# A two-layer gMLP and attention trunk on one core: the first norm's weights spread by matmuls, the root table loaded first, row tiles turned sooner, attention in another order

## What is computed

```python
for l in range(DEPTH):
    h = rms_norm(x, pre_mix_g[l])
    z = h @ w_in[l]                       # columns: u | v | q | k | value
    uv = gelu(z[..., :o_q])               # u, v_g = halves of uv
    y_a = gmlp_mixer(u, v_g, ...)         # u * (W_s LN(v) + b), blocks of 128, chunk mask
    y_b = diff_attention(q, k, v, ...)    # rotary, two softmaxes, a = p0 - lam * p1
    mix = concat([y_a, y_b]) @ w_out[l]
    x = x + rms_norm(mix, post_mix_g[l])
    h = rms_norm(x, pre_ffn_g[l])
    gu = h @ w_gate_up[l]
    y = (silu(gate) * up) @ w_down[l]
    x = x + rms_norm(y, post_ffn_g[l])
```

## Time and profile before

| | |
|---|---|
| median of 3 runs | 1178.06 us (1175.87 to 1179.88) |
| the profiled execution | 1176.28 us, of which its span is 1174.5 us |
| granted TensorE clock, mean over the span | 0.993 |
| PE busy | 1125.2 us (96%), 5309 matmuls |
| ACT, POOL, DVE busy | 463.9, 474.5, 304.4 us |

### The profile page before, as it was taken

One profiled execution on the slowest core, in us unless ns is written; L12 is line 12 of the kernel. 1 busy time (PEld: TensorE's weight loads), 2 busy tenths in 40 slices (PEclk: granted clock), 3 DMA queues, 4 the chain that ended last, 5 costly groups with the idle time before them and its releaser, 6 DMA issues.

```text
span 1174.5 us, 13010 instructions
## 1 busy us (share of the span) xinstructions
PE 1125.2 (96%) x5309; PEld 921.5 (78%) x5309; DVE 304.4 (26%) x534; ACT 463.9 (39%) x833; POOL 474.5 (40%) x210
## 2 busy tenths in 40 slices
PE   4989999899999999999999999998999999999998
PEld 3767767798888888888877776788888888888886
DVE  5264543511111101000243546344111011110002
ACT  5546575532223223222346557744232232231312
POOL 4424245334344344444434233542343443454440
PEclk9999999999999999999999999998999999999999
DMA  8322212314332332332234221122323323323311
GB/s 277 108 72 72 71 57 72 90 55 125 108 98 83 107 108 84 114 104 93 72 111 141 60 84 54 54 86 59 112 86 108 107 80 101 108 90 108 105 57 72
DMA packets 142592, 110.17 MB, mean 94 GB/s; under 512 B 3506, under 2 KB 119748, under 8 KB 142532
## 3 DMA queue, kind: packets, MB, share of 16 engines
q1 hardware_dynamic: 142388, 108.81, 30.1%
q10 hardware_dynamic: 144, 0.52, 0.1%
HBM read 107.23 MB, written 2.10 MB: 93 GB/s over the span
## 4 chain that ended last, share of the span: by engine, by line
PE 85%; DVE 6%; ACT 6%; issue 2%; DMA 0%; POOL 0%; DVEq 0%; ACTq 0%; POOLq 0%
PE banks L409 27%; PE banks L411 26%; PE banks L410 26%; ACT swap L901 2%; PE banks L468 2%; PE banks L498 1%; DVE o_rows L1223 1%; PE banks L418 1%; PE banks L483 1%; DVE scratch L1099 1%; DVE nmx L1181 1%; PE banks L512 1%; DVE cw L1190 1%; ACT junk L806 0%; DMA x_rows<-in_x_dram 0%
## 5 line engine op out<-in xcount | busy, mean ns | idle before, releaser
L374 POOL TENSOR_TENSOR w_lo<-raw,w_hi 128x1024 fp32r<-128x1024 f32 x182 | 438.1, 2419 | 639.7 <-ACT w_hi L798 639.5
L409 PE MATMUL banks<-xg_hi,w_hi 128*128 128x512 f32 (+1 forms) x896 | 346.4, 387 | 0.0
L411 PE MATMUL banks<-xg_lo,w_hi 128*128 128x512 f32 (+1 forms) x896 | 342.9, 383 | 0.0
L410 PE MATMUL banks<-xg_hi,w_lo 128*128 128x512 f32 (+1 forms) x896 | 342.6, 382 | 0.0
L798 ACT ACTIVATE w_hi<-raw 128x1024 fp32r<-128x1024 f32 x182 | 186.9, 1054 | 174.3 <-PE banks L411 174.0
L409 PEld LDWEIGHTS banks<-xg_hi,w_hi 128*128 128x128 f32 x896 | 169.1, 189 | 34.1 <-issue 2.2
L411 PEld LDWEIGHTS banks<-xg_lo,w_hi 128*128 128x128 f32 x896 | 168.9, 188 | 33.1
L410 PEld LDWEIGHTS banks<-xg_hi,w_lo 128*128 128x128 f32 x896 | 168.9, 189 | 31.5
L409 PE MATMUL banks<-w_hi,hid_hi 128*128 128x512 f32 x352 | 137.2, 390 | 0.0
L410 PE MATMUL banks<-w_hi,hid_lo 128*128 128x512 f32 x352 | 137.0, 389 | 0.0
L411 PE MATMUL banks<-w_lo,hid_hi 128*128 128x512 f32 x352 | 137.0, 389 | 0.0
(11 more groups left out here) (123 smaller groups left out, 1042.3 us busy)
## 6 DMA issues: line engine op xcount, KB each, us to landing
raw<-in_w_gate_up_dram SPq DMA_DIRECT2D x88, 512.0 KB, 3.8
raw<-in_w_down_dram SPq DMA_DIRECT2D x44, 512.0 KB, 3.5
raw<-in_w_in_dram SPq DMA_DIRECT2D x40, 512.0 KB, 3.8
raw<-in_w_out_dram SPq DMA_DIRECT2D x16, 512.0 KB, 3.5
x_rows<-in_x_dram SPq DMA_DIRECT2D x4, 512.0 KB, 8.5
out_dram<-x_rows SPq DMA_DIRECT2D x8, 256.0 KB, 2.0
trig<-in_rope_dram SPq DMA_DIRECT2D x2, 512.0 KB, 4.4
gpost<-in_post_mix_g_dram SPq DMA_DIRECT2D x2, 512.0 KB, 4.9
```

What stands on the lines that cost most here:

```text
L374: tt(lo, raw_half(l, c, h), hi.bitcast(F32), ALU.subtract).then_inc(w_ready, 1)
L409: mm(o, stat[0], mov[0], start=first, stop=False)
L410: mm(o, stat[1], mov[0], start=False, stop=False)
L411: return mm(o, stat[0], mov[1], start=False, stop=last)
```

## The change

It has four parts.

**1. The start.** The gains of the first norm are loaded as one row of 4 KB into an unused part of `v_att`. Two matmuls with a row of ones spread it to 128 partitions in PSUM, and DVE and ACT copy one half each into `gpre`. ACT takes one root of a constant first. PE turns the identity 40 times before it turns row tile 0. Then `vg` is made for row tile 0 alone before tile 1 is turned, and the order of `xg_high` and `xg_low` follows.

**2. Boundaries.** Tile 0 is turned within `out_rows(2)` or `down_rows(2)` and no longer after it, and tile 1 after 3 of 8 parts (or 2 of 4) of the last row tile and no longer after 5 (or 3). ACT and DVE bring `xg_high` and `xg_low` of tiles 0 and 1 around `residual(2)`.

**3. The factor `cw`** is written by a tensor_scalar instruction with two factors given per row, where a scalar_tensor_tensor was used.

**4. Attention in another order,** on PE, ACT and DVE, in both layers.

The diff, cut to its core:

```diff
+            pe.wait_ge(consts_ready, 2)
+            pe.wait_ge(gain0_landed, 16)
+            for half in range(2):
+                mm(bank[3 + 4 * half][:, :], ones[0:1, :], gpre_row[:, half * HALF:(half + 1) * HALF],
+                   start=True, stop=True).then_inc(gain0_spread, 1)
+
             pe.wait_ge(ident_ready, 1)
+            for n in range(40):
+                tr(b_tr[0][:, n % ST, :], ident[:, :], ident[:, :])
             turn_rows(0, 0)
-            turn_rows(0, 1)
...
-                vg(0, (0, 1))
+                if l == 0:
+                    vg(0, (0,))
+                    turn_rows(group, 1)
+                    vg(0, (1,))
+                else:
+                    vg(0, (0, 1))
                 turn_rows(group, 2)
...
-                for r in range(3):
+                for r in range(2):
                     out_rows(l, r)
-                turn_rows(group, 0)
+                out_rows(l, 2, lambda: turn_rows(group, 0))
                 out_rows(l, 3, lambda: turn_rows(group, 1))
...
-            act.dma_start(gpre[:, :], pre_mix_g[0].partition_broadcast(P)).then_inc(gpre_landed, 16)
+            act.dma_start(gpre_row, pre_mix_g[0:1, :]).then_inc(gain0_landed, 16)
...
             act.wait_ge(consts_ready, 2)
+
+            fn(root_of_eps[:, :], eps[:, :], ACT.Sqrt)
+            act.wait_ge(gain0_spread, 2)
+            fn(gpre[:, HALF:D], bank[7][:, :], ACT.Copy).then_inc(gain0_copied, 1)
...
                 for r in range(ST):
+                    if r == 2:
+                        xg_low(group, 0)
                     residual(b, r)
-                    if r >= 2:
-                        xg_low(group, r - 2)
+                    if r == 2:
+                        xg_low(group, 1)
...
-                    stt(cw[:, n:n + 1], rinv[:, n, 1:2], neg_lam[:, l:l + 1], psumr[:, n, 0:1], ALU.mult, ALU.mult)\
+                    ts(cw[:, n:n + 1], rinv[:, n, 1:2], neg_lam[:, l:l + 1], psumr[:, n, 0:1], ALU.mult, ALU.mult)\
                         .then_inc(cw_ready, 1)
...
                 qk_half(l, 2, lower)
+                qk_half(l, 2, upper)
                 scores(l, 0)
-                qk_half(l, 2, upper)
                 qk_half(l, 3, lower)
```

More of the change, by code:

```diff
@@ L439, in wide_part, with value_rows @@
                 return last
-            def value_rows(l, c, c0, rows, into, row_ready, row_done):
-                for h in range(2):
+            def value_rows(l, c, c0, rows, into, row_ready, row_done, halves=range(2)):
+                for h in halves:
                     k0 = 4 * (c - c0) + 2 * h
@@ L652, in _ @@
                 qk_half(l, 3, upper)
-                def va(c, rows):
-                    value_rows(l, c, C_VA, rows, [0, 1, 0, 1], att_row_ready, va_done)
                 scores(l, 2)
                 turn(l, 0)
-                va(C_VA, (0, 1))
+                va(C_VA, 0, (0, 1))
+                va(C_VA, 1, (0, 1))
+                scores(l, 3)
+                turn(l, 1)
+                va(C_VA + 1, 0, (0, 1))
+                va(C_VA + 1, 1, (0, 1))
+                scores(l, 4)
                 pe.wait_ge(qk_rotated, 8 * l + 4)
@@ L685, in _ @@
                 scores(l, 7)
+                gate(l, 0)
                 qk_half(l, 5, lower)
@@ L698, in _ @@
                 scores(l, 9)
-                gate(l, 2)
+                gate(l, 3)
                 qk_half(l, 7, upper)
-                scores(l, 10)
                 turn(l, 8)
                 u_half(l, 0, lower)
+                scores(l, 10)
                 turn(l, 9)
@@ L710, in _ @@
                 scores(l, 12)
-                gate(l, 3)
                 u_half(l, 1, upper)
@@ L845, in boundary @@
                 for r in range(ST):
+                    if r == 2:
+                        xg_high(group, 0)
                     if r == ST - 1:
@@ L971, in _ @@
                 high(l, 4, 1)
+                swapped(2)
                 exponentials(0)
-                swapped(2)
                 high(l, 5, 0)
                 exponentials(1)
+                copy_turned(0)
+                high(l, 5, 1)
+                exponentials(2)
                 swapped(3)
-                high(l, 5, 1)
-                copy_turned(0)
-                exponentials(2)
+                copy_turned(1)
+                exponentials(3)
+                copy_values(0)
+                copy_values(1)
                 act.wait_ge(ws_turned, l + 1)
                 fn(wsT[:, :, :], b_tr[O_BANK][:, :, :], ACT.Copy).then_inc(ws_copied, 1)
-                copy_turned(1)
-                copy_values(0)
-                exponentials(3)
-                copy_values(1)
+                exponentials(4)
+                high(l, 6, 0)
                 copy_turned(2)
-                high(l, 6, 0)
-                exponentials(4)
                 high(l, 6, 1)
+                exponentials(5)
+                high(l, 7, 0)
                 copy_turned(3)
                 take_heads(0)
-                high(l, 7, 0)
-                exponentials(5)
                 copy_values(2)
@@ L1001, in _ @@
                 swapped(4)
+                exponentials(7)
                 high(l, 8, 0)
-                exponentials(7)
                 copy_turned(6)
@@ L1006, in _ @@
                 high(l, 8, 1)
+                copy_turned(7)
                 swapped(5)
-                copy_turned(7)
-                exponentials(8)
                 take_heads(3)
                 swapped(6)
+                exponentials(8)
                 high(l, 9, 0)
@@ L1025, in _ @@
                 copy_u(1)
+                copy_turned(11)
                 high(l, 10, 1)
@@ L1029, in _ @@
                 u_gelus(1)
-                copy_turned(11)
                 copy_turned(12)
@@ L1141, in boundary @@
                 xg_low(group, 3)
-            dve.wait_ge(gpre_landed, 16)
+            dve.wait_ge(gain0_spread, 1)
+            copy(gpre[:, 0:HALF], bank[3][:, :]).then_inc(gain0_copied, 1)
+            dve.wait_ge(gain0_copied, 2)
             norm_row(0, 0)
+            xg_low(0, 0)
             norm_row(0, 1)
-            xg_low(0, 0)
+            xg_low(0, 1)
             norm_row(0, 2)
-            xg_low(0, 1)
             norm_row(0, 3)
@@ L1277, in _ @@
                 maxima(7)
+                add_terms(0)
                 rotate(4)
@@ L1280, in _ @@
                 rotate(5)
-                add_terms(0)
+                add_terms(1)
                 maxima(8)
-                add_terms(1)
+                add_terms(2)
                 rotate(6)
@@ L1286, in _ @@
                 combine(8)
-                add_terms(2)
-                maxima(10)
+                add_terms(3)
                 combine(9)
                 rotate(7)
+                maxima(10)
                 combine(10)
                 maxima(11)
+                combine(11)
                 maxima(12)
-                combine(11)
-                add_terms(3)
+                combine(12)
                 maxima(13)
-                combine(12)
                 combine(13)
```

77 lines of the change are left out of this document (42 added, 35 removed).

## The result

| | before | after |
|---|---|---|
| median | 1177.21 us (4 runs, 1175.87 to 1179.88) | 1151.78 us (4 runs, 1150.98 to 1153.24) |
| ratio after to before, 95% interval | | 0.9783 (0.9769 to 0.9798) |
| the profiled execution and its span | 1176.28, 1174.5 us | 1152.33, 1150.5 us |
| granted clock, mean | 0.993 | 0.996 |

The account below looks back on a forecast made before the run. PE bounds it, busy 1125.2 of 1174.5 us. Boundaries 15.7 plus attention 12.5 minus start 3.0 gives 25.2 off 1176.3: 1151.1; 1.8 added for the median makes 1152.8, stated as 1152.5, range 1144 to 1163.

Parts of the forecast that it names:

- Boundaries, -15.7: Three group boundaries: PE's waits for low parts and the half clock after two go, gaining 5.9 + 2.9 + 6.9 us.
- The margins that were worked out: Boundaries: tile 1's low part ready before PE needs it, 1.0 us to spare at the first, 1.5 between the layers.
- The clock's part: Boundaries: 4.4 us of the gain, from half clock no longer following two waits; called the less sure.
- Attention, -12.5: Both layers: waits of 14.2 us and 1.6 of half clock go; new waits of 0.9 and 2.4 come.
- cw, nothing: Attention's factor cw: 0.22 us per instruction in the new form, mostly off PE's path, worth nothing by itself.
- The start, +3.0: Start of the kernel: a loss of 1.6 us up to turning 2 plus 1.4 for half clock after PE's idling.
- T: Start: the time row tile 0 is turned, from 9.4 to 13.6 us, taken as 11.0; it was 11.62.
- turning 2: Start: the turning of row tile 2, forecast to end at T + 17.6, 28.6 us; before, 27.0.
- (b), no clock from 40 turnings: Start: the 40 turnings don't raise the clock, so the loss is 8 us and not 3; 1157.5 us; chance 0.22.
- (c), attention given back: Attention: five late hand-overs in each layer, 1.2 us each, lose 12 us; 1164.5 us; chance 0.16.
- (d), cw still caught: Attention: POOL catches the new cw, 2.1 us each; slower if 12 or more of 32 on PE's path; chance 0.04.
- the limits set: Wrong if turning 2 comes before 26 or after 33 us, a boundary still waits, or attention's waits exceed 8 us.

Follow-up runs that it names:

- e3: The kernel before with the changed boundaries alone; 1159.38 us, ratio to before 0.9855.
- e9: The kernel before with the new tensor_scalar form of cw alone; 1175.19 us, ratio to before 0.9986.
- e8: The changed kernel with the old scalar_tensor_tensor form of cw; 1153.94 us, ratio to before 0.9792.
- e1: The changed kernel with the start of the kernel before; attention, boundaries and cw as changed; 1145.39 us, ratio to before 0.9736.
- e2: The changed kernel without the 40 turnings of the identity; 1148.17 us, ratio to before 0.9757.
- e5: The changed kernel with the second high part of the first weights moved on ACT ahead of turned tile 0's copies; 1146.40 us, ratio to before 0.9732.
- e4: The kernel before with attention's new order on PE, ACT and DVE alone, cw in its old form; 1167.93 us, ratio to before 0.9919.

## Why the prediction was right, step by step

The time forecast was 1152.5, the measured one 1151.78. That it is as near as that is luck twice over. Terms were off in opposite ways: start 3.8 us too good, attention 2.1 too bad, boundaries 0.5 too bad. And the forecast for a profiled run was 1151.1, which came out at 1152.33; 1.8 were added because the median of the kernel before stood that much above its profiled run, and that of the changed kernel stands 0.6 below its own. Which term failed:

- **Boundaries, -15.7: right.** Measured -16.2, and in e3 the same three stages without the other parts. The margins that were worked out (1.0 and 1.5 us) held: no wait at any of the three. The clock's part, called the less sure, is in the sum.
- **Attention, -12.5: right in kind, 2.1 too small.** All waits that were to go have gone, and the two that were to come are there: `par` 0.94 for 0.9, `turn(8)` 1.14 twice for 1.2, from the chain of `add_terms(2)` one step earlier. PE's waits in attention, all added up, fell from 17.4 to 6.2 us (2.3 + 1.8 + 1.2 + 0.9 in the list above), by 11.2 (forecast 10.9). With the half clock of 1.6 that makes 12.8. The other 1.8, 0.9 in each layer, are in no wait of the trace, and no term of the sum held them; the new order puts other matmuls next to each other, but whether that is the cause stays open.
- **cw, nothing: off by about 2 us.** It is 0.27 and not 0.22, and never held by POOL, though 11 of the 32 begin beside one of its instructions, so the type of the instruction did what was said. The value was wrong: PE's path went through held ones in the old order (1.4 in each layer, e9), and would in the new one (0.9 and 0.8, e8). Since the attention term took all waits for combinations as gone, with `cw` at 0.22, that gain stood in its sum under another name. By the second half of the rule quoted from the Trainium skill, "GPSIMD Engine Reference", Specifications (a 2-port mode contends as well), those 11 would have been long if the new form ran in such a mode; none was, and no run here shows its mode.
- **The start, +3.0: the term that failed.** T was 13.41 and not 11.0. Of the 2.4, 0.3 are the landing of the row (3.29 for 3.0), 1.7 the spread (3.75 for 2.0), and 0.4 the turnings (6.5 for 6.0). From T to the end of turning 2 the sum had 17.6, the trace has 19.3 (32.71 - 13.41). The chain is the one described (high part behind tile 0, POOL, DVE's two scalings held), but links that the sum had at the full clock ran at half of it: the six products ahead of tile 1 took 1.9 for 1.4, the turning of tile 1 1.91 for 1.0, the second half of tile 2 1.11 for 0.66. So turning 2 ended 5.7 us later than before (32.7 for 27.0), where 1.6 were forecast. Behind it the half clock added 1.15 up to tile 3, for which 1.4 had been put in. So two steps were mis-sized: T by 2.4, by the spread above all (its own upper bound, 13.6, held the value), and the chain behind T by 1.7. e1 prices the whole at 6.4 to 7.0, e2 the turnings at 3.2, e5 the order on ACT at 5.9; the last two can't be added, for each holds the 1.6 of the second half clock.
- **(b), no clock from 40 turnings: refuted.** The pace doubled during them. The Trainium skill, "TensorE: Matmul & The Clock Gate", Part 4, has it that transposes don't count as busy for the clock; the 21 turnings in 2.0 us, with nothing but turnings on PE for 4 us ahead of them, disagree. The loss that (b) was to bring came all the same, by other ways: 6.8 of its 8.
- **(c), attention given back: no.** Three kinds of hand-over were late and not five in each layer: `par`, `turn(8)`, and the last heads' scaling (0.91 in each layer for 0.46). **(d), cw still caught: no.** e8, with all the old ones back, costs 1.7, so even then it would not have decided.

Of the limits set, attention's waits were to stay under 8 us and are 6.2; turning 2 was to come before 33 and ended at 32.7.

## What to carry to other kernels

Compare two orders of one program at points that have the same work behind them: a stage that nobody touched then reads the same to 0.1 us as long as no half clock falls into it, and each part of a change gets its own number from one profile. At a start, ask what stands ahead of the first link of each chain on its queue: here one high part that waited for nothing cost 5.9 us because it stood behind a copy that did (1.6 of them by a half clock that the delay brought). The turnings that warmed PE up held tile 0 back by 3.25 us and gave back 1.7, because the rest of PE's speed was hidden under waits. Where a tile is made of two SBUF inputs beside a busy POOL, and one of them stands in PSUM anyway, it is best read there.

## What the runs showed of the hardware that was not expected

- **The length of a wait does not tell the clock behind it.** After PE waits of 2.54 and 2.55 us at the same place it was 0.53 in one program and 1.00 in the other; after 1.99 and 2.00, 0.50 in e4 and 1.00 in e8. After 2.89 it was 1.00 in the kernel before, and after 2.90 it was half in e4 and e9. After 4.21 a slow stretch followed all six times (kernel before, e4, e9). What decides is not shown by these runs; a half clock of 3.4 us cost 1.5 to 1.7 us each time.
- **A row spread by matmul is slow.** One fp32 matmul of 1x512 shows as two in the trace; the four took 3.75 us, 0.94 each, at the start of the program.
- **Two SBUF inputs beside POOL cost both sides, and the one that begins later pays.** DVE's pair took 4.71 and 4.19 us when it began while POOL worked, but 1.42 when it began first (9.33, POOL from 10.06). POOL's 128x1024 subtraction took 2.91 us there, and 2.39 where DVE was idle. With one input from PSUM neither was held: 1.41 and 2.36. The Trainium skill, "GPSIMD Engine Reference", Specifications, names two SBUF inputs as what contends; the trace agrees, and these numbers are the price.
- **The form that is slower at its best is the safer one.** The new `cw` took 0.27 us in all 32 instructions of every trace that had it; the old one took 0.22 at the least and 2.15 to 2.34 at most.
